# Strassen's products for two chunks of four feed forward stages of a two-block transformer kernel

## The reference, cut to what matters

```python
def swiglu(x, w_in, w_out):
    a, b = jnp.split(x @ w_in, 2, axis=-1)      # w_in [1024, 2*2816]
    return (jax.nn.silu(a) * b) @ w_out          # w_out [2816, 1024]
...
h = h + FFN_RES * rms_norm(swiglu(rms_norm(h, g[0]), w_in, w_out), g[1])
...
mod = jnp.dot(jax.nn.silu(c), w_ada) + b_ada     # w_ada [1024, 6*1024]
shift1, scale1, gate1, shift2, scale2, gate2 = jnp.split(mod, 6, axis=-1)
```

## Time and profile before

| | |
|---|---|
| median of 3 runs | 1418.01 us (1417.1 to 1418.36) |
| the profiled execution's own time | 1416.94 us |
| its span in the profile | 1415.1 us |
| granted TensorE clock, share of full speed | 0.999 |
| busy: PE, DVE, ACT, POOL | 1401.8, 956.5, 731.7, 160.1 us |
| stage 2, from the first chunk of tok 1 to the next stage's first transposes | 314.14 to 492.63 us |
| stages 3, 5, 7 begin about | 492, 790, 1230 us |
| DMA | 288.24 MB, 204 GB/s over the span |

### The profile page before, as it was taken

One profiled execution on the slowest core, in us unless ns is written; L12 is line 12 of the kernel. 1 busy time (PEld: TensorE's weight loads), 2 busy tenths in 40 slices (PEclk: granted clock), 3 DMA queues, 4 the chain that ended last, 5 costly groups with the idle time before them and its releaser, 6 DMA issues.

```text
span 1415.1 us, 19090 instructions
## 1 busy us (share of the span) xinstructions
PE 1401.8 (99%) x7327; PEld 1147.2 (81%) x7327; DVE 956.5 (68%) x1307; ACT 731.7 (52%) x1050; POOL 160.1 (11%) x242
## 2 busy tenths in 40 slices
PE   9999999999999999999999999999999999999997
PEld 7888888688888888888878888888877788888886
DVE  6666567886676667665787757755568566786654
ACT  6444455564443445543665545445655634655542
POOL 1600010000000000000172100000542110011000
PEclk9999999999999999999999999999999999999999
DMA  9585755256876778868544688764845355588551
GB/s 318 199 253 198 262 203 207 68 171 207 251 242 215 231 228 265 252 210 264 187 150 148 203 210 256 255 211 140 238 160 197 121 178 179 171 242 211 178 209 59
DMA packets 234857, 288.24 MB, mean 204 GB/s; under 512 B 37076, under 2 KB 156672, under 8 KB 234768
## 3 DMA queue, kind: packets, MB, share of 16 engines
q1 hardware_dynamic: 232160, 281.48, 61.6%
q0 software_dynamic: 2208, 5.24, 1.8%
q10 hardware_dynamic: 400, 0.31, 0.1%
HBM read 282.80 MB, written 4.20 MB: 203 GB/s over the span
## 4 chain that ended last, share of the span: by engine, by line
PE 95%; DVE 2%; issue 1%; ACT 1%; POOL 0%; POOLq 0%; ACTq 0%; DVEq 0%
PE ps L706 29%; PE ps L709 28%; PE ps L707 28%; PE pst L974 1%; PE pst L1155 1%; DVE wlo L532 1%; PE pst L1468 1%; PE ps L813 0%; PE ps L812 0%; PE ps L811 0%; PE ps L1415 0%; ACT whi L521 0%; PE ps L679 0%; PE pst L1782 0%; PE pst L2355 0%
## 5 line engine op out<-in xcount | busy, mean ns | idle before, releaser
L532 DVE TENSOR_TENSOR wlo<-raw,whi 128x1024 fp32r<-128x1024 f32 (+2 forms) x468 | 558.2, 1224 | 257.7 <-ACT whi L521 255.9
L521 ACT ACTIVATE whi<-raw 128x1024 fp32r<-128x1024 f32 (+2 forms) x468 | 467.8, 1040 | 244.2 <-PE ps L709 97.4
L706 PE MATMUL ps<-whi,xh 128*128 128x512 f32 (+4 forms) x1406 | 551.5, 392 | 1.6 <-ACT xh L1013 0.6
L707 PE MATMUL ps<-wlo,xh 128*128 128x512 f32 (+4 forms) x1406 | 541.1, 385 | 0.0
L709 PE MATMUL ps<-whi,xl 128*128 128x512 f32 (+4 forms) x1406 | 532.7, 385 | 0.0
L706 PEld LDWEIGHTS ps<-whi,xh 128*128 128x128 f32 x1406 | 263.9, 188 | 60.6 <-issue 4.7
L709 PEld LDWEIGHTS ps<-whi,xl 128*128 128x128 f32 x1406 | 263.9, 188 | 53.6
L707 PEld LDWEIGHTS ps<-wlo,xh 128*128 128x128 f32 x1406 | 264.2, 188 | 49.8
L706 PE MATMUL ps<-whi,gh 128*128 128x512 f32 x440 | 172.0, 391 | 0.0
L707 PE MATMUL ps<-wlo,gh 128*128 128x512 f32 x440 | 171.2, 389 | 0.0
L709 PE MATMUL ps<-whi,gl 128*128 128x512 f32 x440 | 153.4, 389 | 0.0
(11 more groups left out here) (306 smaller groups left out, 956.0 us busy)
## 6 DMA issues: line engine op xcount, KB each, us to landing
raw<-in_ffn_w_in_dram SPq DMA_DIRECT2D x174, 512.0 KB, 5.3
raw<-in_ffn_w_out_dram SPq DMA_DIRECT2D x40, 1024.0 KB, 5.5
raw<-in_w_in_dram SPq DMA_DIRECT2D x26, 1024.0 KB, 4.8
adat<-in_w_ada_dram SPq DMA_DIRECT2D x96, 256.0 KB, 2.8
raw<-in_hyb_w_in_dram SPq DMA_DIRECT2D x10, 1024.0 KB, 5.1
raw<-in_gla_w_in_dram SPq DMA_DIRECT2D x10, 1024.0 KB, 5.2
raw<-in_w_ffn_down_dram SPq DMA_DIRECT2D x10, 1024.0 KB, 5.0
raw<-in_w_ffn_gate_dram SPq DMA_DIRECT2D x18, 512.0 KB, 3.9
```

The lines of the kernel that those rows point to most:

```text
L521: e.activation(split_of(whi, j), raw_of(j), ACT.Copy).then_inc(*whi_made.up(j))
L532: e.tensor_tensor(split_of(wlo, j), raw_of(j), split_of(whi, j).bitcast(F32), ALU.subtract).then_inc(*wlo_made.up(j))
L706: e.matmul(ps[:, 0:n], a, whi_of(j, k), start=first and k == 0, stop=False)
L707: last = e.matmul(ps[:, 0:n], a, wlo_of(j, k), start=False, stop=False)
```

## The change

Stages 2, 3 and 5 take two chunks by Strassen's products too, and in all four stages the pair is chunks 9 and 10 in place of 8 and 9. Chunk 8 is then the one turned alone. Every product moves one chunk later, and p4 is the last piece before the down projection. There, chunk 8 is turned at down sub-tile 0, silu and gate of the pair follow, and the pair is turned at sub-tile 3. The first two down sub-tiles do tok 0 first. The five sums of x blocks are spread over chunk 2's four steps and chunk 3's first, their splits over the last two steps of chunk 3. The tiles of w_ada skip the units loaded by POOL. Their twelve rounds stand 9.6 units apart rather than 10, and each round's sending, reading and sum come one unit earlier in the round. Two gate rows are written to memory by 8 DMAs of 128 elements each in place of one of 1024, and the first of the two is read back 6 units later than before.

```diff
-        STRASSEN = (7,)
-        PAIR = 8
+        STRASSEN = (2, 3, 5, 7)
+        PAIR = 9
...
-                return (0, 1, "p1", 2, "p2", 3, "p5", 4, "p6", 5, "p3", 6, "p7", 7, "p4", 10)
+                return (0, 1, 2, "p1", 3, "p2", 4, "p5", 5, "p6", 6, "p3", 7, "p7", 8, "p4")
...
-        ada_units = [u for st in (0, 2, 3, 5) for u in range(U0[st] + (8 if st == 0 else 0), U0[st + 1])]
+        ada_units = [u for st in (0, 2, 3, 5) for u in range(U0[st] + (8 if st == 0 else 0), U0[st + 1]) if u not in home]
         ada_tiles, ada_sent, ada_read, ada_summed = {}, {}, {}, {}
         for c in range(12):
+            i = min(10 * c, c * (len(ada_units) - 13) // 11)
             for k in range(8):
-                ada_tiles[ada_units[10 * c + k]] = c, k
-            ada_sent[ada_units[10 * c + 11]] = c
-            ada_read[ada_units[10 * c + 12]] = c
-            ada_summed[ada_units[10 * c + 13]] = c
+                ada_tiles[ada_units[i + k]] = c, k
+            ada_sent[ada_units[i + 10]] = c
+            ada_read[ada_units[i + 11]] = c
+            ada_summed[ada_units[i + 12]] = c
...
-        def dve_sx(e, st):
-
-            def whole(z):
-                return z[:, :].bitcast(F32).rearrange("p (k n) -> p k n", k=8)[:, :, 0:P]
+        def dve_sx(e, st, step):
+
             a11, a12, a21, a22 = (sum_of(name) for name in ("p6", "p3", "p7", "p5"))
-            e.wait_ge(*squares.at(("h", st, 1), 1))
-            e.wait_ge(*xlo_made.at(st, 1, 3 if st == 7 else 1))
-            e.tensor_tensor(junk[:, :].rearrange("p (k n) -> p k n", k=8), whole(xh), whole(xl), ALU.add
-                            ).then_inc(*summed.up(st, "x", 0))
-            e.tensor_tensor(a22, a21, a22, ALU.subtract).then_inc(*summed.up(st, "x", "p5"))
-            e.wait_ge(*summed.at(st, "x", "p5"))
-            e.tensor_tensor(a21, a11, a21, ALU.subtract).then_inc(*summed.up(st, "x", "p7"))
-            e.wait_ge(*summed.at(st, "x", "p7"))
-            e.tensor_tensor(a11, a22, a11, ALU.subtract).then_inc(*summed.up(st, "x", "p6"))
-            e.wait_ge(*summed.at(st, "x", "p6"))
-            e.tensor_tensor(a12, a12, a11, ALU.add).then_inc(*summed.up(st, "x", "p3"))
-
-        def act_sx(e, st):
+            if step == 0:
+                def whole(z):
+                    return z[:, :].bitcast(F32).rearrange("p (k n) -> p k n", k=8)[:, :, 0:P]
+                e.wait_ge(*squares.at(("h", st, 1), 1))
+                e.wait_ge(*xlo_made.at(st, 1, 3 if st == 7 else 1))
+                e.tensor_tensor(junk[:, :].rearrange("p (k n) -> p k n", k=8), whole(xh), whole(xl), ALU.add
+                                ).then_inc(*summed.up(st, "x", 0))
+            if step == 1:
+                e.tensor_tensor(a22, a21, a22, ALU.subtract).then_inc(*summed.up(st, "x", "p5"))
+            if step == 2:
+                e.wait_ge(*summed.at(st, "x", "p5"))
+                e.tensor_tensor(a21, a11, a21, ALU.subtract).then_inc(*summed.up(st, "x", "p7"))
+            if step == 3:
+                e.wait_ge(*summed.at(st, "x", "p7"))
+                e.tensor_tensor(a11, a22, a11, ALU.subtract).then_inc(*summed.up(st, "x", "p6"))
+            if step == 4:
+                e.wait_ge(*summed.at(st, "x", "p6"))
+                e.tensor_tensor(a12, a12, a11, ALU.add).then_inc(*summed.up(st, "x", "p3"))
+
+        def act_sx(e, st, half):
+            o = slice(half * 1024, (half + 1) * 1024)
             e.wait_ge(*summed.at(st, "x", "p3"))
-            e.activation(sxh[:, :], workx[:, :], ACT.Copy).then_inc(*xhi_made.up(st, "sums"))
-
-        def dve_sx_lo(e, st):
-            e.wait_ge(*xhi_made.at(st, "sums"))
-            e.tensor_tensor(sxl[:, :], workx[:, :], sxh[:, :].bitcast(F32), ALU.subtract).then_inc(*xlo_made.up(st, "sums"))
+            e.activation(sxh[:, o], workx[:, o], ACT.Copy).then_inc(*xhi_made.up(st, "sums", half))
+
+        def dve_sx_lo(e, st, half):
+            o = slice(half * 1024, (half + 1) * 1024)
+            e.wait_ge(*xhi_made.at(st, "sums", half))
+            e.tensor_tensor(sxl[:, o], workx[:, o], sxh[:, o].bitcast(F32), ALU.subtract
+                            ).then_inc(*xlo_made.up(st, "sums", half))
...
+                if key[1] in STRASSEN and i == 0:
+                    continue
+                if key[1] in STRASSEN and i == 1:
+                    one(held.pop(0), 1)
...
+        def alone(st):
+            return PAIR - 1 if st in STRASSEN else 10
...
-                acc.n += 4
+                acc.n += 2
...
-                if i == 2:
+                if i == (0 if st in STRASSEN else 2):
                     pe_hid(e, st)
+                if st in STRASSEN and i == 3:
+                    pe_hid_two(e, st, PAIR)
...
-        COMBINE = {2: "p1", 5: "p6", 7: "p7"}
+        COMBINE = {(3, 1): "p1", (6, 2): "p6", (8, 2): "p7"}
+        SX_AT = [(2, 0), (2, 1), (2, 2), (2, 3), (3, 0)]
+        SXLO_AT = [(3, 2), (3, 3)]
...
                 act_begin(e, JD[st] + i)
-                if i == 2:
-                    act_ghi(e, st, 10)
+                if i == (0 if st in STRASSEN else 2):
+                    act_ghi(e, st, alone(st))
+                if st in STRASSEN and i == 0:
+                    act_silu_pair(e, st, 0)
+                    act_silu_pair(e, st, 1)
+                if st in STRASSEN and i == 3:
+                    act_ghi(e, st, PAIR)
...
+            pool_strassen(e, 2)
             pool_open(e, 3)
+            pool_strassen(e, 3)
             pool_gla(e)
             pool_open(e, 5)
+            pool_strassen(e, 5)
...
+        gate_piece = {u0 + b: (which, b) for which, u0 in ((2, U0[5] + 10), (5, U0[6] + 8)) for b in range(8)}
...
-                if u in (U0[5] + 10, U0[6] + 8):
-                    i, which = (0, 2) if u < U0[6] else (1, 5)
-                    e.wait_ge(*mod_made.at(2 * which + 1))
-                    e.dma_start(gate_rows[i].rearrange("(b p) -> p b", p=P), modc[:, which * 8:which * 8 + 8],
-                                allow_slow_non_contiguous=True).then_inc(*s_gates.up(which))
-                if u == U0[6] + 10:
+                if u in gate_piece:
+                    which, b = gate_piece[u]
+                    if b == 0:
+                        e.wait_ge(*mod_made.at(2 * which + 1))
+                    e.dma_start(gate_rows[which // 5][b * P:(b + 1) * P].rearrange("(p o) -> p o", o=1),
+                                modc[:, which * 8 + b:which * 8 + b + 1], allow_slow_non_contiguous=True
+                                ).then_inc(*s_gates.up(which))
+                if u == U0[6] + 16:
```

More of the change, by code:

```diff
@@ L568, in pool_strassen @@
             pool_product(e, st, "p5", True)
-            e.wait_ge(*xlo_made.at(st, "sums"))
+            e.wait_ge(*xlo_made.at(st, "sums", 1))
             pool_product(e, st, "p3", False)
@@ L1115, in act_silu_pair @@
             if tok == 0:
-                e.wait_ge(*hid_turned.at(st, PAIR - 2))
+                e.wait_ge(*hid_turned.at(st, PAIR - 1))
             e.activation(pair_of(hidx, tok, 256), both(acc.of(st, "ba"[tok])), ACT.Silu,
@@ L1126, in dve_gate_pair, with turn_of @@
                                    ).then_inc(*gated.up(st, PAIR, tok))
-        def turn_of(c):
+        def turn_of(st, c):
+            if st in STRASSEN:
+                return PAIR - 1 if c == PAIR - 1 else PAIR if c >= PAIR else c - c % 2
             return c if c == 10 else c - c % 2
+        def alone(st):
+            return PAIR - 1 if st in STRASSEN else 10
         def pe_hid(e, st):
-            ps = tb.next(("hid", st, 10), (glo_made, st, 10))
+            c = alone(st)
+            ps = tb.next(("hid", st, c), (glo_made, st, c))
             for done in tb.freed:
                 e.wait_ge(*done)
-            e.wait_ge(*gated.at(st, 10, 1))
+            e.wait_ge(*gated.at(st, c, 1))
             for j in range(2):
@@ L1140, in pe_hid @@
                                        hid[0][:, tok * 512 + j * P:tok * 512 + (j + 1) * P], ident)
-            last.then_inc(*hid_turned.up(st, 10))
+            last.then_inc(*hid_turned.up(st, c))
         def pe_hid_two(e, st, c):
@@ L1155, in pe_hid_two @@
                     last = e.transpose(pst[:, half * 512 + b * 64:half * 512 + (b + 1) * 64],
-                                       hid[(c + n) % 2][r, tok * 512 + j * P:tok * 512 + (j + 1) * P], ident[r, r])
+                                       hid[n][r, tok * 512 + j * P:tok * 512 + (j + 1) * P], ident[r, r])
             last.then_inc(*hid_turned.up(st, c))
@@ L1166, in act_ghi @@
             e.wait_ge(*hid_turned.at(st, c))
-            if c == 10:
-                e.activation(gh[:, 5120:5632], tb.of("hid", st, c)[:, :], ACT.Copy).then_inc(*ghi_made.up(st, c))
+            if c == alone(st):
+                e.activation(gh[:, c * 512:(c + 1) * 512], tb.of("hid", st, c)[:, :], ACT.Copy).then_inc(*ghi_made.up(st, c))
             else:
@@ L1173, in dve_glo @@
             e.wait_ge(*ghi_made.at(st, c))
-            if c == 10:
```

(36 more changed lines are left out.)

12 lines of the change are left out of this document (2 added, 10 removed).

## The result

The changed kernel takes **1441.3 us** (median of 6 runs, 1435.0 to 1446.2) against 1417.2 us for the kernel before on the same chip, a ratio of 1.0165 with an interval of 1.0138 to 1.0192. The forecast was 1411.4 us, so the sign was wrong. The profiled execution took 1437.29 us, with a span of 1435.2 us. That is 20.1 us over the span before, and 26.7 us over the span of 1408.5 us that the sum gave.

The account below looks back on a forecast made before the run. The prediction took PE, busy for 99% of the span, as the bound. It summed -8.2 us for removed matmuls and +1.6 us for stage 5's opening to -6.6 us, from 1418.01 to 1411.4 us, range 1409.0 to 1417.0.

Parts of the forecast that it names:

- the gate rows: Writing a row by eight short DMAs gains nothing by itself and only takes a burst away from the fuller stretch; no cost.
- The matmuls removed: Stages 2, 3 and 5 lose 12 matmuls each, 36 at 0.2267 us on PE: -8.2 us.
- The sum of round 8 in the opening: Stage 5's opening: five small DVE operations ahead of the scaling delay PE by +1.6 us.
- DVE at chunk ends: Late gates in stages 2, 3 and 5: taken as nothing, at most 0.9 us at two ends a stage, 5.4 us.
- rival 2: Gates late at chunk ends, or the tail's load late: 1413.9 to 1420.8 us, typically 1416; chance 0.18.
- rival 3: DMA becomes the bound in the three new stages, kernel slower, 1435 us; sign: ACT waits for DMAs; chance 0.09.
- The rounds of w_ada: Tiles stay where PE never saw them, except round 8's sum, moved into stage 5's opening: +1.6 us.
- The tail: Four stages, chunk 8 to down projection, p4 alone: costs nothing, upper end 1 us a stage if a load lands late.
- DMA: Extra weight loads in Strassen stages: taken as nothing, though about 2.0 us short per chunk, up to 6 us a stage.
- The warning on GpSimd's DMAs: GpSimd DMAs can stand still while VectorE holds the shared port; against moving three stages' weights to POOL; not priced.
- Rivals 1 and 4: 1: stage 5's opening sum hidden, 1409.8 us, chance 0.13. 4: stalls eat each new stage's 2.7 us, 1418 us, 0.08.

Follow-up runs that it names:

- e2: The kernel before, with only the gate rows written in eight pieces and the first row read back 6 units later: 1430.0 us.
- e1: The changed kernel with each gate row written by one DMA of 1024 elements, at the unit of the first of the eight: 1423.4 us.
- e5: The changed kernel with both gate rows written in stage 6 by one DMA each, none in stage 5: 1417.8 us.
- e8: e7 with the reads and sums of w_ada rounds 2 and 3 also moved later: 1410.5 us, ratio 0.9957 to the kernel before.
- e3: The changed kernel with the first gate row's eight pieces moved from stage 5 to stage 4: 1427.0 us.
- e11: e8 plus eight extra DMAs in stage 5, each writing 512 contiguous bytes from one partition: 1411.2 us.
- e7: e5 with w_ada round 7 started one unit earlier and read and summed later, and round 8's sum moved past stage 5's opening: 1413.9 us.
- e6: The changed kernel with the first gate row in stage 5 as two DMAs of 512 elements, the second by one in stage 6: 1422.7 us.
- e10: e8 with the first gate row written in stage 5 by four DMAs of 256 elements, the second by one in stage 6: 1425.8 us.

## Why the prediction was wrong

**The step that failed** is the gate rows: "so eight short ones instead gain nothing by themselves. They only take a burst away from the stretch that gets fuller." It was costed at nothing. In the old kernel it measured +13 us (e2), in the changed one +18 (1441.3 against e1's 1423.4), and with the one write of stage 5 gone too, +23.5 (against e5). The 12.4 us to landing (the middle of two writes, 11.0 in stage 5 and 13.8 in stage 6) and DVE's wait of 5.94 were read as one burst whose size goes with its bytes. The window 839 to 845.5 of the kernel before, shown above, had the answer, and the prediction did not read it. The DMAs were occupied throughout and moved 78 GB/s. No upper bound was set for eight of them. A bound from the row, 5.94 us each time, is 48 us less what is absorbed, and would have made the sign open.

**The matmuls removed, -8.2 us**: right. Undisturbed stages shortened by 2.7 us each: stage 3 in e8 (178.5 to 175.8) and stage 5 in e3, e5, e8 and e11 (177.13 to 174.44). The silu starts of the changed stage 3 lie 13.60 us apart, as forecast (557.79 to 571.39), and 14.5 where a turn of hidden values stands between (571.39 to 585.88).

**The sum of round 8 in the opening, +1.6 us**: right, at 1.5. PE waited 1.50 us for L1026, and DVE did its five small operations (792.53 to 794.06) straight ahead of the scaling. e7 removed it.

**DVE at chunk ends, costed at 0, upper end 5.4**: stage 2 lost 5.1 us in one place, not at six ends. In the changed kernel, DVE's timeline at the end of chunk 3 of stage 2 reads:

```profile
358.49 1.22 DVE L533 TENSOR_TENSOR wlo<-raw,whi 128x1024 fp32r<-128x1024 f32 x1
359.63 0.74 DVE L627 SCALAR_TENSOR_TENSOR adaacc<-adat,scol,adaacc 128x512 f32<-128x512 f32 x1
360.29 1.22 DVE L613 TENSOR_TENSOR sxl<-work,sxh 128x1024 fp32r<-128x1024 f32 x1
361.42 0.87 DVE L1113 SCALAR_TENSOR_TENSOR hid<-ps,st,hid 128x256 f32<-128x256 f32 x2
```

No idle time stands before the gate, which is the sign that the prediction named for rival 2, and PE waited for it:

```profile
361.95 0.50 PE L715 MATMUL ps<-whi,xh 128*128 128x512 f32 x1 [2.33 <-DVE hid L1113]
```

But the sign named for rival 3 is there as well, a little earlier in the same chunk. ACT stood idle for loads, and DVE behind it for 2.54 and 1.07 us:

```profile
350.43 2.01 ACT L522 ACTIVATE whi<-raw 128x1024 fp32r<-128x1024 f32 x2 [5.50 <-DMA raw<-in_ffn_w_in_dram]
355.12 1.06 ACT L522 ACTIVATE whi<-raw 128x1024 fp32r<-128x1024 f32 x1 [2.20 <-DMA raw<-in_ffn_w_in_dram]
```

The second of these loads took an ordinary 5.2 us, but it was sent only at 349.40, after SP had waited 8.1 us for DVE's addition of an earlier tile of w_ada, which frees the buffer of the tile that stands ahead of it in the queue. So work added on DVE can come back as a late load, a loop that the prediction's sum of DVE's time for each chunk doesn't contain. No run takes this loop apart from the rest of the stop.

The other half of the loss I had not priced at all. After the stop, the granted clock is 0.53 for 3.5 us (the fifth window of the result), so near the lower of its two levels, and the stage's matmuls are busy 2.2 us longer. The rounds of w_ada were counted for the openings and not for this end. e8, which only moved reads and sums, took away 3.7 us of it.

**The tail, costed at 0, upper end 1 a stage**: 1.2 us in stage 3 alone, by the way the prediction left out. SP's send of round 7 (4.93 us, at 609.02) stood between the loads of the two down units. e7 removed it.

**DMA, costed at 0**: right for the loads. The windows at 0.81 to 0.82 and 243 GB/s lose nothing with the three adding loads in them. The prediction quoted the Trainium skill (SBUF — State Buffer, "A bandwidth-pool intuition that's wrong") for about 358 GB/s from memory to one core. The stream runs at 0.68 of that, and the trace agrees that it did not bound as such. But the figure is no ceiling here: the core moved 363 GB/s for 3.5 us (fifth window of the result). The warning on GpSimd's DMAs that the prediction took from the Trainium skill (SBUF — State Buffer, "Who interferes with whom") did not show: e8's stage 5 has all of those DMAs, and PE has no wait in it.

Rivals 1 and 4 did not occur. Rival 2 did in part, in stages 2 and 3, and within its bounds (5.1 us of 5.4 and 1.2 of 4), but it is the smaller part of the miss: with no single-element write in stage 5 the kernel took 1417.8 us (e5), 6.4 over the forecast, where the changed kernel is 29.9 over. With the costs of the gate rows and of the rounds taken away, the products do what the count of matmuls said: 1417.2 - 8.2 + 1.9 still lost in stage 2 = 1410.9 us, and e8 measured 1410.5.

What stays open: why a write of single elements slows the loads of the other queue as well. It wasn't tried whether the source partitions, the 4-byte targets or the number of packets do it, since e11 changed all three (from 839 to 842 us e1 has 1032 packets under 512 bytes, e11 has 16). In e1 1013 of them start within the first of these microseconds, so it is the loads behind the write that are slow, for a reason that no run here shows. Stage 2 of e8 still loses 1.9 us; 1.41 of it is the gap named above.

## What to carry to other kernels

A small DMA can cost more than its bytes and its time to landing. Ask for the GB/s in the window behind it together with the DMAs' share. If the rate is low for its share, price one such stretch for each DMA as the upper bound, and don't split it: two halves gained nothing here, four and eight pieces lost 15.5 and 20.4 us. A change that takes the slack out of a stage makes every stall that was hidden there visible, so list those stalls first (here a DVE wait of 5.94 us) and price each with the cover gone. When a recurring task is spread by an index rule, check where each of its steps lands after the plan changes: eight moved steps were worth 7.3 us here (e5 to e8).

## What the runs showed of the hardware

- A write of 256 to 1024 single 4-byte elements from 128 partitions to memory was followed by 6 to 7.5 us at 41 to 86 GB/s for the core (before, e1, e6, e10), that is 64 to 183 for a full share of the DMAs, where e8's stage 5 as a whole has 296. With eight writes of 128 in the changed kernel, the loads on both queues landed late (12.1 and 13.2 us, where e8 has 6.9 and 10.9 in the same window). Eight writes of 512 contiguous bytes in their place left the stage at 174.44 us, unchanged (e11).
- In the changed kernel a stop of PE of 2.33 us was followed by 3.5 us at a granted clock of 0.53. A stop of 1.50 us in the opening of stage 5 was followed by nothing of the kind: the 6.4 us after it (795.56 to 802.00) ran at 1.00, as did the 3.6 us after e8's stop of 1.41. In stage 5 of the changed kernel two stops of 15.2 us together went with 5.2 us more of matmul time, at a mean clock of 0.96.
